# A hybrid decoder layer with 32 experts: the sixth expert's weights loaded in pieces, and the first expert's products put ahead of the second expert's turn

## What is computed

```python
def _back(x, mods, o_attn, o_conv, gate_a, gate_b, w_pa, w_pb, w_o, g_ffn,
          w_rg, b_rg, w_re, b_re, w_gate_e, w_up_e, w_down_e):
    gate1, shift2, scale2, gate2 = mods
    merged = jax.nn.sigmoid(gate_a) * (o_attn @ w_pa) + jax.nn.sigmoid(gate_b) * (o_conv @ w_pb)
    x = x + gate1 * (merged @ w_o)
    h = _rmsnorm(x, g_ffn) * (1 + scale2) + shift2
    return x + gate2 * _hier_moe(h, w_rg, b_rg, w_re, b_re, w_gate_e, w_up_e, w_down_e)
```

## Time and profile before

| | before |
|---|---|
| runs | 776.17 us median of 3 (775.86 to 776.75) |
| the profiled execution | 776.93 us, span 775.2 us |
| TensorE products busy | 714.5 us (92%) |
| TensorE weight loads busy | 538.0 us (69%) |
| VectorE, ScalarE, GpSimd busy | 322.9, 165.7, 126.8 us |
| DMA | 202.88 MB, mean 262 GB/s |
| chain that ended last | TensorE 80%, DMA 8%, VectorE 4%, issue 4% |

### The profile page before, as it was taken

One profiled execution on the slowest core, in us unless ns is written; L12 is line 12 of the kernel. 1 busy time (PEld: TensorE's weight loads), 2 busy tenths in 40 slices (PEclk: granted clock), 3 DMA queues, 4 the chain that ended last, 5 costly groups with the idle time before them and its releaser, 6 DMA issues.

```text
span 775.2 us, 12402 instructions
## 1 busy us (share of the span) xinstructions
PE 714.5 (92%) x5097; PEld 538.0 (69%) x5097; DVE 322.9 (42%) x722; ACT 165.7 (21%) x323; POOL 126.8 (16%) x194
## 2 busy tenths in 40 slices
PE   3989999999999999999999999999999968888973
PEld 1689899789898989999997455665565545545431
DVE  3342322226688763322234765525333421222246
ACT  4332212211254532112110112111111110110101
POOL 3400001210014011100000100123333332223111
PEclk9999999999999999999999999999999998999997
DMA  9844466865144339721105962789999999999983
GB/s 335 333 164 164 164 243 257 284 256 184 55 148 158 120 130 376 301 97 56 55 28 174 424 281 81 247 332 415 415 414 411 410 414 416 418 414 418 404 351 123
DMA packets 41668, 202.88 MB, mean 262 GB/s; under 512 B 8514, under 2 KB 8698, under 8 KB 25860
## 3 DMA queue, kind: packets, MB, share of 16 engines
q1 hardware_dynamic: 31488, 175.55, 57.7%
q0 software_dynamic: 9456, 26.14, 9.4%
q10 hardware_dynamic: 668, 0.40, 0.2%
HBM read 188.60 MB, written 21.72 MB: 271 GB/s over the span
## 4 chain that ended last, share of the span: by engine, by line
PE 80%; DMA 8%; DVE 4%; issue 4%; ACT 1%; SPq 1%; POOL 1%; DVEq 0%; POOLq 0%; ACTq 0%
PE bank L1765 30%; PE bank L2020 14%; PE bank L1965 7%; PE bank L2042 6%; PE bank L1908 4%; DMA arena<-in_w_ada 2%; PE bank L2013 2%; PE bank L1905 2%; PE bank L1662 2%; PE bank L1801 2%; DMA arena<-y_scratch 2%; PE bank L1864 2%; DMA arena<-h_scratch,arena_b 1%; DMA arena<-in_w_in 1%; PE bank L1705 1%
## 5 line engine op out<-in xcount | busy, mean ns | idle before, releaser
L1765 PE MATMUL bank<-h_parts,w_parts 128*128 128x260 f32 x2112 | 265.9, 285 | 2.2 <-issue 1.5
L1765 PEld LDWEIGHTS bank<-h_parts,w_parts 128*128 128x128 f32 x2112 | 256.5, 188 | 11.3 <-issue 9.7
L2020 PE MATMUL bank<-arena,arena_b 128*64 128x256 f32 x704 | 87.4, 404 | 14.6 <-issue 12.3
L2020 PEld LDWEIGHTS bank<-arena,arena_b 128*64 128x64 f32 x704 | 56.2, 145 | 40.4 <-issue 15.7
L1131 DVE TENSOR_TENSOR w_parts<-arena,w_parts 128x1024 fp32r<-128x1024 f32 x46 | 56.2, 1221 | 58.8 <-ACT w_parts L950 58.6
L1492 DVE TENSOR_TENSOR arena_b<-bank,arena_b 128x128 f32<-128x128 f32 x32 | 9.3, 292 | 123.8 <-ACT arena_b L1062 123.7
L950 ACT ACTIVATE w_parts<-arena 128x1024 fp32r<-128x1024 f32 x46 | 48.4, 1053 | 49.2 <-DMA arena<-in_w_in 34.5
L1965 PE MATMUL bank<-arena,arena_b 128*128 128x512 f32 x128 | 56.7, 597 | 0.0
L876 POOL DMA_INDIRECT y_scratch<-arena_b x30 | 31.2, 1041 | 149.0 <-DVE arena_b L1519 140.9
L2042 PE MATMUL bank<-arena,arena_b 128*64 128x512 f32 x176 | 42.3, 594 | 2.3 <-DVE arena_b L1498 2.3
L1965 PEld LDWEIGHTS bank<-arena,arena_b 128*128 128x128 f32 x128 | 23.8, 190 | 28.2 <-issue 28.1
(11 more groups left out here) (324 smaller groups left out, 828.6 us busy)
## 6 DMA issues: line engine op xcount, KB each, us to landing
arena<-in_w_gate_up SPq DMA_DIRECT2D x44, 1024.0 KB, 28.0
arena<-in_w_in SPq DMA_DIRECT2D x46, 512.0 KB, 6.9
arena<-in_w_ada SPq DMA_DIRECT2D x22, 1024.0 KB, 7.4
arena<-in_w_down SPq DMA_DIRECT2D x20, 1024.0 KB
arena_b<-in_w_gate_up SPq DMA_DIRECT2D x20, 1024.0 KB
arena_b<-in_w_down SPq DMA_DIRECT2D x20, 512.0 KB
arena_b<-in_x_prompt SPq DMA_DIRECT2D x8, 512.0 KB, 5.3
y_scratch<-arena_b POOLq DMA_DIRECT2D x1, 4096.0 KB, 25.5
```

Of the source, the lines that this page charges most:

```text
L1765: ins = pe.matmul(ps[s][:, 0:HALF], w_parts[:, n % 2, wp, k], h_parts[:, hp, k, s * HALF:(s + 1) * HALF], start=(k == 0 and hp == 1), stop ...
L2020: ins = pe.matmul(ps[2 + b][R * hh:R * hh + R, 0:2 * P], hTe[:, b, c * P + jj * R:c * P + jj * R + R], w_gu[slot][jj][:, c, :, hh * P:(hh ...
```

## The change

SyncE's list is reordered around the residual blocks, the semaphore `s_xw` is split into three (the samples' block; blocks 0 and 1; blocks 2 and 3), and two lines of TensorE's loop are changed.

- After the writes of the first three blocks SyncE issues the first down half of expert 5 (when the samples' block is stored), then, when `s_h2` is 6 and blocks 0 and 1 are stored, the first gate and up half of expert 5. The write of the fourth block follows.
- The second gate and up half is issued after expert 4's, when blocks 2 and 3 are stored, ahead of expert 6's down weights. The second down half follows when `s_rt` is 5. The waits on `s_sq` and `s_hg[0]` are gone.
- Expert 1's rows are turned after expert 0's products. For experts 1 to 27 the turn of the next expert stays ahead of the products.

```diff
-            for n in range(4):
+            for n in range(3):
                 keep_x(n)
+            sp.wait_ge(s_xw[0], 16)
+            load_down(5, 5, 0)
+            sp.wait_ge(s_h2, 6)
+            sp.wait_ge(s_xw[1], 32)
+            load_gate_up(5, 5, 0)
+            keep_x(3)
             sp.wait_ge(s_wom[0], 5)
...
             sp.wait_ge(s_h2, 10)
             load_gate_up(4, 4, 0)
             load_down(4, 4, 0)
+            sp.wait_ge(s_xw[2], 32)
+            load_gate_up(5, 5, 1)
             for part in range(2):
                 load_down(6, 6, part)
-            sp.wait_ge(s_xw, 16 * 5)
-            sp.wait_ge(s_sq, 15)
             sp.wait_ge(s_rt, 5)
-            sp.wait_ge(s_hg[0], 16)
-            for half in range(2):
-                load_gate_up(5, 5, half)
-                load_down(5, 5, half)
+            load_down(5, 5, 1)
...
             for e in range(NE):
-                if e + 1 < NE and e < SOON:
+                if 0 < e < SOON:
                     turn_rows(e + 1, e + 1, 16 * ((e + 1) // EUN + 1))
...
-                if e + 1 < NE and e >= SOON:
+                if e == 0 or SOON <= e < NE - 1:
                     turn_rows(e + 1, e + 1, 16 * ((e + 1) // EUN + 1))
```

More of the change, by code:

```diff
@@ L460, in hybrid_step @@
         s_added = sem("s_added")
-        s_xw = sem("s_xw")
+        s_xw = [sem(f"s_xw{i}") for i in range(3)]
         s_xl = sem("s_xl")
@@ L614, in keep_x @@
                 if i == 4:
-                    sp.dma_start(xs_d, x[0:TS, i]).then_inc(s_xw, 16)
+                    sp.dma_start(xs_d, x[0:TS, i]).then_inc(s_xw[(n + 1) // 2], 16)
                 else:
-                    sp.dma_start(x_d[i * P:i * P + P], x[:, i]).then_inc(s_xw, 16)
-            for n in range(4):
+                    sp.dma_start(x_d[i * P:i * P + P], x[:, i]).then_inc(s_xw[(n + 1) // 2], 16)
+            for n in range(3):
                 keep_x(n)
+            sp.wait_ge(s_xw[0], 16)
[4 more added lines that the diff above has]
+            keep_x(3)
             sp.wait_ge(s_wom[0], 5)
@@ L1071, in _ @@
                 if e == 12:
-                    act.wait_ge(s_xw, 16 * 5)
+                    act.wait_ge(s_xw[0], 16)
                     gate_rows = mod_d[1:1 + TS, 5 * D:6 * D].rearrange("b (c d) -> b c d", c=16)
```

## The result

| | before | after |
|---|---|---|
| median | 775.9 us (18 runs, 772.12 to 777.28) | 778.09 us (18 runs, 776.05 to 782.46) |
| ratio | | 1.004, 95% interval 1.0026 to 1.0055 |
| the profiled execution | 776.93 us, span 775.2 | 779.88 us, span 778.1 |
| TensorE products busy | 714.5 us | 714.5 us |
| DMA | 202.88 MB | 202.88 MB |

The changed kernel is slower by 0.4%, some 3 us (0.26 to 0.55%); the medians lie 2.2 us apart. It does the same work: the same bytes, the same products. So the time is a matter of when.

What follows compares the result with a forecast made beforehand. The stream of weights was taken to bound the end. Expert 7's stream start summed as 523.38 + 0.2 + 0.1 + 2.4 + 1.7 = 527.8 against 526.65, +1.1 on the 776.17 median: 777.3 us, range 774.8 to 779.2.

Steps and rivals of the forecast that it cites:

- the side that I gave 0.32: Whole kernel: slower than before by more than about 0.2% (1.55 us); chance 0.32.
- The stream of weights bounds the end, and the 7.6 us collapse to expert 7's start: Expert loop: 7.6 us of early bytes gain only the shift of expert 7's stream start, 526.65 us before.
- The early pieces cost nothing: Residual blocks: 1.57 MB of expert 5, issued at about 459 and 464 us into a 37 GB/s stretch, cost nothing.
- The last h_scratch write, +0.1: Write that releases the gathers: lands 0.1 us later behind 1.57 MB more loads; bounds 0 and 0.6.
- The first gather, +2.4: Gather before TensorE's first turn: starts 2.4 us late behind q1's loads; bounds 0.8 and 5.0.
- From issue to flow, +1.7: Expert 7's loads: 1.7 us from issue to flow, no longer hidden behind expert 6; bounds 0.8 and 2.6.
- The order, +0.2: TensorE's loop start: products 0.6 us earlier, moved turn 0.5 later, table load exposed; expert 1's end net 0.2 us later.
- The clock: Expert 0's products after 3 us of idle TensorE: 5.36 us instead of 3.67, adding 1.7; left out of the sum.
- the gather held by the queue: Rival at the first gather: it pays over 2.85 us, or the lower clock adds 1.7; slower, up to +3.7; chance 0.32.

Runs made afterwards that it cites:

- e2: The kernel before with only TensorE's new order (expert 1's rows turned after expert 0's products); 775.59 us, ratio 1.0013 to before.
- e10: The changed kernel with TensorE's old order, the rest of expert 5 and expert 6's down weights behind the first gather; 774.16 us, ratio 0.9988 to before.
- e12: The kernel before with the 20 weighing products put behind expert 1's products instead of expert 0's; 776.55 us, ratio 1.0009 to before.
- e11: e6 with the 20 weighing products put behind expert 1's products instead of expert 0's; 775.32 us, ratio 1.0002 to before.
- e13: e1 with the weighing products put behind expert 1's products; 777.61 us, ratio 1.0028 to before.
- e6: The changed kernel with TensorE's old order and the half of expert 5 not loaded early behind the first gather; 772.61 us, ratio 0.9956 to before.
- e5: The kernel before without SyncE's wait for the first gather, so all of expert 5 is issued ahead of it; 779.01 us, ratio 1.0046 to before.
- e1: The changed kernel's loads with TensorE's old order (expert 1's turn ahead of expert 0's products); 776.26 us, ratio 1.0013 to before.
- e3: The changed kernel, but the half of expert 5 not loaded early waits for the first gather; 774.32 us, ratio 0.9987 to before.
- e4: The changed kernel with 20 filling products on TensorE ahead of the first turn instead of 8; 778.3 us, ratio 1.004 to before.
- e9: The changed kernel with 14 filling products on TensorE ahead of the first turn instead of 8; 777.97 us, ratio 1.0021 to before.

## Why the prediction was right, and where not

The direction and the range held; 778.09 lies within 774.8 to 779.2. But the forecast of +1.1 us had put the likeliest case within 0.2%, and it came out on the side that I gave 0.32. The range held because it reached into that rival; in the sum, the gather's overestimate (0.5) hid part of what was missing. That the sum came within 2 us is partly luck. By its own steps:

- *The stream of weights bounds the end, and the 7.6 us collapse to expert 7's start.* Right. The stretch from 620 us is unchanged, and in twelve of the fourteen profiles the place in the stream follows expert 7's issue, or q1's backlog where that is as late or later (before, e2, e10, e12). In the other two (e11, e13) it follows what the step left out, expert 7's down load and expert 8's loads behind it.
- *The early pieces cost nothing.* Right for the time: 123 GB/s where there were 37, and e6, which has them, is no slower than before in either job. The `h_scratch` write that they meet, issued at 463.4, lands after 6.6 us instead of 2.9, within the 30 us that it had to spare.
- *The last h_scratch write, +0.1.* Measured +0.6, the upper bound given.
- *The first gather, +2.4.* Measured +1.9. The mechanism was right, a late start in a loaded queue: the first records stand in 511.5 to 512 us, where 512.0 was forecast. e5 shows the price growing with the bytes ahead.
- *From issue to flow, +1.7.* About 1.5.
- *The order, +0.2.* Measured +1.0 in the company of the late gather (e1 against the changed kernel, +28.2 and +29.2). The 0.6 us won in the sum are not there, since the second gather has landed by then; the moved turn and the exposed table load are there, near their prices (0.7 and 0.3; the sum had 0.8 for both).
- *The clock.* The term that failed by being left out of the sum: +1.7, the largest but the gather's. I had it as the second way of the rival "the gather held by the queue", at 1.7, and it was this that decided: the gather paid 1.9, short of the 2.85 which that rival asked of it alone. The reason I gave against it, that TensorE was busy nearly throughout ahead of its idle time, was true (10.16 of the 10.5 us from 499.5 on) and did not keep the clock. It comes with the late gather in either order (5.36 us in e1, 5.7 in e5), and with the new order even where the gather is in time (4.9 and 5.1 us for expert 1 in e2 and e3, one profile each). In e4 and e9, where filling products close the gap, expert 0's products keep it; so the gap is its cause there.
- *The sum with what was measured*: 24.58 + 0.6 + 1.9 - 0.6 + 1.7 + 1.0 = 29.2 us behind the last write, and 1.5 to the flow, 30.7, against 27.9: 2.8 us late. The count at 220 us says 3.1, the spans say 2.9.

The shares of the two halves of the change are not quite additive. By the stream the loads alone are 1.7 us late, the order alone 0.2, both 3.1; by the ratios 0.13%, 0.13% (both intervals reach no change) and 0.4%. By this reading the order's cost is hidden while q1 has 5.2 MB to move at the start of the loop, and the change took just that work away.

## What to carry to other kernels

When a transfer is moved ahead of a bound stream, ask what the stream's next piece waits for: here the 7.6 us of moved bytes were worth only the distance to the next slot's release, and that release hung on a chain of one gather, two turns and 2 x 3.7 us of products. A wait on a small transfer in a queue's program, which looks like an order of data only, may be what keeps the small transfer from meeting the large ones; take the bytes that are gone by then, and leave the rest behind it. And a gap on TensorE can be priced twice, once for itself and once for the clock of what follows it: 3.1 us cost 1.7 more here, while the two gaps of 0.6 us in the kernel before cost no clock.

## What the runs showed of the hardware that I had not expected

- The time of one small indirect gather (0.14 MB) against what stood in the other queue: 3.0 us to its consumer with 2.6 MB issued from 9 us ahead and nearly gone, 4.9 with 4.2 MB, 7.1 with 5.8 MB, 8.0 to 8.3 in the full stream. The last three are more than the 3.8 us that the equal turns of the earlier trace rows give. The first records came 1.6, 3.2 and 4.1 us or more after the issue in the first three.
- The granted clock: 3.1 us without work and then 0.7 us more ahead of expert 0's products gave 0.66 of full speed over the 5 us behind them, that is mostly the lower of the two levels of 1.2 and 2.4 GHz, and 5.36 us for 3.67 us of products, although TensorE had worked 10.16 of the 10.5 us up to 510. In e2 no gap ahead of them was longer than 0.7 us on TensorE, and expert 1's products still fell to 4.8 us. In e9 the filled gap moved the fall to the next expert. These traces don't tell where the clock will fall, and each of these runs was profiled once; that it may fall where no gap was longer than 0.7 us is what to reckon with.
